# Pivot's tiles added on GpSimd ahead of one product, one square tile added on VectorE, the last tile stored from SyncE

## The reference, cut to what matters

```python
def layernorm(x, g, b):
    mu = jnp.mean(xf, axis=-1, keepdims=True)
    var = jnp.mean(jnp.square(xf - mu), axis=-1, keepdims=True)
    y = (xf - mu) * lax.rsqrt(var + EPS)

def conformer_conv(x, norm_g, pw1_w, pw1_b, dw_w, dw_b, ln_g, ln_b, pw2_w, pw2_b):
    a, b = jnp.split(rmsnorm(x, norm_g) @ pw1_w + pw1_b, 2, axis=-1)
    h = a * jax.nn.sigmoid(b)
    h = lax.conv_general_dilated(h, dw_w[:, None, :], window_strides=(1,),
        padding=[(CONV_WIDTH - 1, 0)], ..., feature_group_count=h.shape[-1]) + dw_b
    h = jax.nn.silu(layernorm(h, ln_g, ln_b))
    return h @ pw2_w + pw2_b
```

## Time and profile before

| | us |
|---|---|
| median of 3 runs (lowest, highest) | 1037.01 (1036.83, 1037.03) |
| the profiled execution, its device time | 1036.92 |
| its span, first to last instruction | 1035.2 |
| TensorE busy | 1017.5 (98%) |
| VectorE busy | 714.2 (69%) |
| ScalarE busy | 540.3 (52%) |
| GpSimd busy | 91.7 (9%) |

### The profile page before, as it was taken

One profiled execution on the slowest core, in us unless ns is written; L12 is line 12 of the kernel. 1 busy time (PEld: TensorE's weight loads), 2 busy tenths in 40 slices (PEclk: granted clock), 3 DMA queues, 4 the chain that ended last, 5 costly groups with the idle time before them and its releaser, 6 DMA issues.

```text
span 1035.2 us, 15770 instructions
## 1 busy us (share of the span) xinstructions
PE 1017.5 (98%) x6374; PEld 872.3 (84%) x6374; DVE 714.2 (69%) x1123; ACT 540.3 (52%) x846; POOL 91.7 (9%) x143
## 2 busy tenths in 40 slices
PE   8998999999999999999999999999999999999997
PEld 8976888888889957888888889999779988888885
DVE  5998866666667696657766678748756457656654
ACT  6336545455454596555545553545655445444442
POOL 4000390000010131000000021000000000000000
PEclk9999999999999999999999999999999999999999
DMA  9983656666636404755766646554245345665631
GB/s 267 250 203 103 200 176 194 203 198 179 200 82 212 156 1 123 224 163 169 219 202 183 202 133 216 173 163 164 82 163 178 107 148 177 191 204 176 201 125 41
DMA packets 189327, 174.71 MB, mean 169 GB/s; under 512 B 13028, under 2 KB 164708, under 8 KB 189255
## 3 DMA queue, kind: packets, MB, share of 16 engines
q1 hardware_dynamic: 187280, 169.67, 54.2%
q10 hardware_dynamic: 1398, 3.12, 0.9%
q0 software_dynamic: 576, 0.92, 0.3%
HBM read 171.76 MB, written 1.93 MB: 168 GB/s over the span
## 4 chain that ended last, share of the span: by engine, by line
PE 88%; DVE 6%; ACT 4%; issue 1%; POOL 0%; DMA 0%; ACTq 0%; POOLq 0%; DVEq 0%
PE bank L1982 15%; PE bank L1984 15%; PE bank L1983 15%; PE bank L2050 11%; PE bank L2054 11%; PE bank L2053 5%; PE bank L2051 5%; DVE split_lo L1167 2%; PE bank L2234 2%; DVE xn L1184 1%; ACT xn L740 1%; PE bank L2434 1%; DVE v L1685 1%; PE bank L2006 1%; PE bank L2650 1%
## 5 line engine op out<-in xcount | busy, mean ns | idle before, releaser
L1167 DVE TENSOR_TENSOR split_lo<-raw,split_hi 128x2048 fp32r<-128x2048 f32 (+1 forms) x159 | 356.5, 2247 | 140.7 <-ACT split_hi L700 140.4
L700 ACT ACTIVATE split_hi<-raw 128x2048 fp32r<-128x2048 f32 (+1 forms) x159 | 297.5, 1874 | 88.7 <-PE bank L1984 82.2
L2050 PE MATMUL bank<-xn,split_hi 128*128 128x512 f32 x480 | 190.5, 397 | 0.7 <-DVE xn L1184 0.7
L2054 PE MATMUL bank<-xn,split_hi 128*128 128x512 f32 x480 | 189.9, 396 | 0.0
L1982 PE MATMUL bank<-xn,split_hi 128*128 128x256 f32 (+2 forms) x496 | 143.1, 289 | 2.3 <-DVE xn L1184 1.6
L1983 PE MATMUL bank<-xn,split_hi 128*128 128x256 f32 (+2 forms) x496 | 140.2, 283 | 0.0
L1984 PE MATMUL bank<-xn,split_lo 128*128 128x256 f32 (+2 forms) x496 | 140.1, 283 | 0.0
L2053 PE MATMUL bank<-xn,split_lo 128*128 128x256 f32 x480 | 133.6, 278 | 0.0
L2051 PE MATMUL bank<-xn,split_lo 128*128 128x256 f32 x480 | 133.2, 277 | 0.0
L1982 PE MATMUL bank<-split_hi,ffa_hi 128*128 128x512 f32 x320 | 124.9, 390 | 0.0
L1984 PE MATMUL bank<-split_hi,ffa_lo 128*128 128x512 f32 x320 | 124.5, 389 | 0.0
(11 more groups left out here) (344 smaller groups left out, 1342.2 us busy)
## 6 DMA issues: line engine op xcount, KB each, us to landing
raw<-in_ffn_w_in SPq DMA_DIRECT2D x88, 512.0 KB, 5.1
raw<-in_w_ff SPq DMA_DIRECT2D x32, 1024.0 KB, 5.5
raw<-in_ffn_w_out SPq DMA_DIRECT2D x22, 1024.0 KB, 5.0
raw<-in_w_in SPq DMA_DIRECT2D x14, 1024.0 KB, 5.2
raw<-in_w_xkv SPq DMA_DIRECT2D x8, 1024.0 KB, 5.4
raw<-in_a_pw_w SPq DMA_DIRECT2D x12, 512.0 KB, 7.3
raw<-in_a_pw_w SPq DMA_DIRECT2D x4, 1024.0 KB, 9.7
raw<-in_b_w_in SPq DMA_DIRECT2D x4, 1024.0 KB, 5.9
```

Source lines behind the costliest of these rows:

```text
L700: nc.scalar.activation(split_slot[m % SPLITS][0][:, 0:n], raw[c % RAWS][:, 0:n], ACT.Copy).then_inc(split_hi, 1)
L1167: return nc.vector.tensor_tensor(dst, src, hi.bitcast(F32), ALU.subtract)
L2050: mm(whole, hi, xn_both[:, :, kt, :], start=kt == 0, stop=False)
L2054: x = mm(whole, hi, xn_both[:, :, kt, :], start=False, stop=kt == KT - 1)
```

## The change

Three things are moved. The pivot's tiles 2, 3 and 4 are added on GpSimd into `tile_sum`, with a new semaphore `pivot_summed`, and TensorE makes one product of the sum instead of three. Tile 4's squares are added to tile 1's on VectorE, and TensorE's product of them is gone; the product of the added squares now opens bank 1. The store of tile 7 (`CONV_PE[-1]`) goes from GpSimd's queue to SyncE's, behind the shifted copies of tile 6.

```diff
             for c, parts in enumerate(chunks):
                 for ft in conv_at.get(c, []):
+                    if ft == CONV_PE[-1]:
+                        sp.wait_ge(glu_done, ft + 1)
+                        sp.dma_start(u_rows[ft], u[:, ft, :]).then_inc(u_stored[-1], 16)
                     shifted_copies(ft)
...
-            for n, ft in enumerate(CONV_PE):
+            for n, ft in enumerate(CONV_PE[:-1]):
                 pool.wait_ge(glu_done, ft + 1)
                 pool.dma_start(u_rows[ft], u[:, ft, :]).then_inc(u_stored[n], 16)
+
+            pool.wait_ge(conv_out, 2)
+            nc.gpsimd.tensor_tensor(tile_sum, v[:, PIVOT[0], :], v[:, PIVOT[1], :], ALU.add).then_inc(pivot_summed, 1)
+            pool.wait_ge(conv_out, 3)
+            pool.wait_ge(pivot_summed, 1)
+            nc.gpsimd.tensor_tensor(tile_sum, tile_sum, v[:, PIVOT[2], :], ALU.add).then_inc(pivot_summed, 1)
...
             add_to(squares(0, 2), squares(2, 2))
+            add_to(squares(1), squares(4))
...
-            for n, ft in enumerate(PIVOT):
-                te.wait_ge(conv_out, n + 1)
-                x = sum_over(0, v[:, ft, :], n == 0, ft == PIVOT[-1])
-            x.then_inc(stat_done, 1)
+            te.wait_ge(pivot_summed, 2)
+            sum_over(0, tile_sum, True, True).then_inc(stat_done, 1)
             conv(3)
             conv(4)
             te.wait_ge(glu_done, KT)
             te.wait_ge(pads_zero, 2)
-            te.wait_ge(squared, 1)
-            sum_over(1, u[:, 4, PAD:PAD + S], True, False)
...
-            sum_over(1, u[:, 0, PAD:PAD + S], False, False)
+            sum_over(1, u[:, 0, PAD:PAD + S], True, False)
```

More of the change, by code:

```diff
@@ L250, in build_kernel @@
         quad_done = sem("quad_done")
+        pivot_summed = sem("pivot_summed")
         u_stored = [sem(f"u_stored{i}") for i in range(len(CONV_PE))]
```

## The result

| | before | after |
|---|---|---|
| median of 20 runs each (lowest, highest) | 1037.06 (1036.7, 1038.87) | 1038.59 (1037.42, 1041.13) |
| ratio after / before (95% interval) | | 1.0015 (1.0009, 1.0021) |
| the profiled execution: time, span | 1036.92, 1035.2 | 1037.51, 1035.8 |
| TensorE busy in its span | 1017.5 | 1016.5 |

The change makes the kernel slower by 1.5 us of 1037, and its executions spread further: 3.7 us against 2.2. TensorE is busy for 1.0 us less, and the time went up all the same. The profiled execution is one of the quickest, 0.6 above its counterpart; the trace shows the part of the loss that every execution has, and the rest needed experiments.

The account below looks back on a forecast made before the run. TensorE, busy 98% of the span, plus its waits was taken as the bound. Its 1.50 saved hides behind tile 7's landing, landing +0.1, rest 0: 1036.92 + 0.1 = 1037.02, median 0.09 above, so 1037.1; range 1036.0 to 1038.4.

Parts of the forecast that it names:

- what holds the last tile: Last tile's start: TensorE's work (80.82) and the copies' landing (80.88) both hold it; TensorE's 1.50 saved is all hidden.
- my 0.78 to 1.56: Pivot sum on GpSimd: duration of each addition in us, scaled from a 1.17 scaling by outputs or by elements read.
- The square addition: Tile 4's squares on VectorE: one more addition of 0.43, covered by 1.06 idle ahead of tile 7's second half.
- Rival 3: VectorE's taps keep GpSimd's additions out, so conv(3) starts late: 2.9 late in all, 1039.9; chance 0.05.
- rival 1: Tile 7's store lands as if alone, 0.4 to 1.06 earlier, or more engines are free: 1036.2; chance 0.19.
- One sign of being wrong: Prediction called wrong if tile 7's copies start before 76.0 or after 76.9, or TensorE waits for the pivot's sum.
- what GpSimd takes from the taps: VectorE's taps beside GpSimd's two additions: 0.35 lost each, 0.70 less 0.18 idle, so tile 7 written 0.52 later.
- This loss hides behind the copies of tile 6 and adds nothing.: Tile 7's store, issued from about 73.5, lands by 75.9, before the 76.4 that full DMA engines allow: no cost.
- a share of 1.05: DMA engines' share from 73.20 to 75.20, read as full until about 75.5, so an earlier store lands no earlier.
- My upper end: Tile 7 written 0.78 late and its store taking 3.2: landing at 76.85, adding 0.5 to 0.8.
- Rival 2: GpSimd holds VectorE for its whole additions, so tile 7 lands 1.1 to 1.9 late: 1038.5; chance 0.15.
- Rival 4: TensorE idles 1.6 more ahead of the last tile and its clock falls; chance 0.05 together with the unforeseen.

Follow-up runs that it names:

- E6: The kernel before with four one-input 128x256 scalings added on GpSimd during the taps, results unread; one run only, the 14 taps took 6.23 us against 5.63.
- E8: Change's store and square, pivot by three products as before, two of tile 7's four copies issued from ScalarE's queue; median 0.62 us below before (-1.3 to 0.5).
- E4: The changed kernel unaltered, run once more for a second trace; median 0.77 us above the kernel before (0.0 to 1.9).
- E7: The changed kernel plus nine unread transposes on TensorE between the convolutions of tiles 6 and 7; median 0.81 us above before (0.1 to 2.0).
- E10: The changed kernel unaltered, one profiled execution meant to catch a slow one; it took 1038.90 us.
- E15: The changed kernel with nine unread transposes in TensorE's wait ahead of the last tile, repeated on another chip; median 0.69 us above before (0.1 to 2.0).
- E2: The kernel before with only the store of tile 7 moved to SyncE's queue; median 0.00 us above before (-0.8 to 1.0).
- E9: As E8, plus one GpSimd addition (tiles 2 and 3) ahead of tile 6's store and two pivot products; median 0.33 us below before (-1.2 to 0.6).
- E13: The changed kernel without the 22 unread transposes ahead of the second product; median 1.80 us above before (1.0 to 2.9).
- E11: The changed kernel unaltered, another single profiled execution meant to catch a slow one; it took 1037.89 us.

## Why the prediction was wrong

I forecast 1037.1, no change, within 1036.0 to 1038.4; it came to 1038.59, 0.19 beyond the range. Two things made it: a delay of tile 7 that I had put at nothing, 0.67 in the trace after, which is the step that failed, and on top a lower clock in part of the executions. Of the first 20 the 13 with a mean clock of 0.998 or 0.999 have a median of 1038.22, 1.2 above before and still inside the range; the seven with 0.997 took it out.

**Right: what holds the last tile.** The landing at 80.88 bounds it, and TensorE's 1.50 saved turns into waiting: `conv(3)` at 72.36, idle time of 0.86 and 1.23 after. The two additions on GpSimd took 0.88 and 1.01, within my 0.78 to 1.56, and TensorE did not wait for them. The square addition was free: VectorE kept 0.77 of idle time. Rival 3 is out, rival 1 too: no store of the whole change landed in less than 3.3. One sign of being wrong came true: the copies of tile 7 start at 77.09, after 76.9.

**Mis-sized: what GpSimd takes from the taps.** I bounded it by 0.48 for each addition and took 0.35, "0.70 - 0.18 = 0.52". It is 0.48 in every trace, so 0.96. The delay of tile 7 is 0.71 and not 0.78, since the slack ahead of its product was 0.26 (from the start of the subtraction ahead of it 2.46 before and 2.20 after, where the idle row says 0.18). The upper end was the right one, but by luck: I had scaled a hold of 0.36 by elements read, and E6 refutes that rule (0.15 where it gives 0.24).

**Failed: "This loss hides behind the copies of tile 6 and adds nothing."** This is the step that turned a loss into no change. I read from a share of 1.05 until 75.20 that the store could not land before 76.4 however early it was issued, and so that one issued 0.5 later would land then too. The first half does not hold beyond that one trace: in E8 the store, issued at 73.02, landed at 75.47. The second assumed that a store waits for the engines' queue and then needs only 2.4 from its issue. In the nine traces that have all three parts (after, E4, E7, E10 to E15) it took 3.3 to 3.9 from issues between 73.73 and 74.53, so its delay is added to its landing. Between E2 and these nine, all with SyncE's store, tile 7 is 0.71 later, chunk 14's issue behind the landing 0.70 to 1.10 later, and the last tile 0.80 to 1.20 later. My upper end was what came: 0.78 late and 3.2 to land gave copies at 76.85, and they start at 77.09, 0.15 of it this execution's own. SyncE's three stores that were not late took 2.45, 3.13 and 3.26 (E8, E2, E9), all less than the nine; why a late one took no less, and rather more, stays open. The copies of tile 6 were no fixed mark either. Their first is issued between 5.15 (E8) and 8.16 (E9) after tile 6's product, before at 7.90. Those of the trace after were issued 1.06 earlier than before and the last landed later, 5.8 after its issue instead of 3.9:

```profile
act<-u_rows SPq DMA_DIRECT2D x1, 141.5 KB, 5.8
```

**Put at nothing without a reason: the product that is gone.** I took its 0.63 as hidden and looked at nothing else that it did. It also took two waits ahead of the landing; without it they are the last tile's, and the last tile starts 0.15 later. That is 0.15 of the 0.67 of the trace after.

**Rival 2's rule.** Had GpSimd held VectorE for its whole instructions, the taps would have lost 1.9. They lost 0.96. The Trainium skill states an exclusive lock, which the instruction that starts first keeps until it has finished (SBUF — State Buffer, Who interferes with whom; for the whole instruction by its Terms). These traces agree in part: an addition on GpSimd lasts longer the longer a VectorE instruction is still running when it starts (0.88 with 0.20, 1.01 with 0.34; 0.92 with 0.24 in E9), and then VectorE stands still. They differ on the end: VectorE gets in 0.19 before the addition ends, and beside a scaling of 0.85 to 1.00 (E6) it waits 0.15 only. The measurement decides. The page's warning pointed the right way all the same, and I gave its direction too little weight.

**Dismissed: the clock.** Rival 4 and everything unforeseen got 0.05. I had judged it by a stretch with 1.78 idle of 6.13 where the clock stayed full. The whole change idles 1.9 to 2.4 ahead of the last tile, in one piece or two, and E13's trace has the fall there, for 1.67. The part common to all traces of the whole change is 0.6 to 1.0, and the 31 executions with a mean clock of 0.998 or more have a median of 1038.06, 0.8 above before; the 1.5 of the first 20 contains seven with less. That the clock is what most executions of the tail suffered rests on these means and on E13: none above 1039.2 of the changed kernel itself was profiled, so where in them the clock fell stays open. Two of the thirteen are not explained by it; waits for landings such as the 0.8 in E10 are left for them.

## What to carry to other kernels

A step taken off an engine gains only if that engine, and not a landing beside it, releases what comes next; look for the next thing that waits for the same landing to see when it came. Elementwise work given to GpSimd is paid by VectorE wherever VectorE runs instructions with two SBUF inputs back to back: price it there at the full hold (0.48 for 256 columns and two inputs here), and put it where VectorE waits for somebody else afterwards. An instruction that is taken away may have carried waits for its neighbours: see where they stand afterwards, since behind a landing they count. And work taken from TensorE ahead of a wait makes idle time, which half clock can follow in part of the executions; a spread that grows is the sign, and the mean granted clock of each execution tells more than the median.

## What the runs showed of the hardware that was not expected

- GpSimd's addition of 128x256 float32 with two inputs holds one VectorE instruction for 0.48, the same with two and with four of them, and VectorE gets in 0.19 before the addition ends; a scaling of the same size with one input holds it for 0.15.
- A 143 KB store took between 2.45 and 4.24 to land in this stretch (2.45 to 3.86 from SyncE's queue, 2.63 to 4.24 from GpSimd's). SyncE issued it 0.03 behind VectorE's write, GpSimd 0.30.
- With two wait instructions of 51 ns in TensorE's queue behind a landing the matmul started 0.22 or 0.23 after the next DMA that waits for this landing; with none, 0.07 or 0.08.
- A stretch at half clock began after 2.22 of idle TensorE, and the 128 passes behind it took 5.37 instead of 3.70; behind 2.38 at the same place in E11, and in all other traces, the clock stayed at 1.00 there.
